# Ends of the two mixture-of-experts layers: a fifth gather buffer, an earlier first scaling, and a last expert tile handled in two column halves

## The reference, cut to what matters

```python
for l in range(DEPTH):                                  # DEPTH = 2
    ...                                                 # attention, residual
    hp = modulate(rms_norm(xp, norm_ffn[l]), sh_m_p, sc_m_p)
    hs = modulate(rms_norm(xs, norm_ffn[l]), sh_m_s, sc_m_s)
    xp = xp + gt_m_p[:, None, :] * hier_moe(hp, *moe_prm)
    xs = xs + gt_m_s[:, None, :] * hier_moe(hs, *moe_prm)
y_prompt = rms_norm(xp, final_norm)
y_sample = rms_norm(xs, final_norm)
```

```python
hid = silu(x @ w_gate[e]) * (x @ w_up[e])               # per expert, width 256
out = sum over the two chosen experts of e_w * (hid @ w_down[e])
```

## Time and profile before

| what | value |
|---|---|
| time, median of 3 executions | 1373.82 us (1367.92 to 1375.38) |
| profiled execution, own time | 1371.09 us |
| its span, first to last instruction | 1369.3 us |
| PE busy in the span | 1256.3 us (92%) |
| DVE, ACT, POOL busy | 583.9, 418.2, 55.8 us |
| mean granted TensorE clock | 0.967 |
| records | 16486 |

### The profile page before, as it was taken

The page is one execution under the profiler, slowest core; times in us unless marked ns, Lnnn a source line. Parts: engine busy times, 40 slices in busy tenths (PEclk is TensorE's granted clock), DMA queues, the critical chain, the costliest instruction groups (busy, mean ns, idle before and its releaser), DMA issues.

```text
span 1369.3 us, 16486 instructions
## 1 busy us (share of the span) xinstructions
PE 1256.3 (92%) x5449; PEld 660.8 (48%) x5449; DVE 583.9 (43%) x1334; ACT 418.2 (31%) x843; POOL 55.8 (4%) x64
## 2 busy tenths in 40 slices
PE   5899899999999999999939996999999999998884
PEld 2455566666664464444414443555444554443331
DVE  1322355444553664222236446677725642212215
ACT  2332344444451121111122336667621211111113
POOL 0102000000000120000020000000000100000002
PEclk9999999999999999999969997999999999999997
DMA  9969999422253067999970004000030469999945
GB/s 375 397 240 414 408 410 414 171 94 94 94 195 134 31 275 263 384 382 371 340 292 9 0 0 190 2 1 1 25 132 31 190 229 374 355 345 343 346 178 216
DMA packets 78545, 299.44 MB, mean 219 GB/s; under 512 B 11817, under 2 KB 29932, under 8 KB 62988
## 3 DMA queue, kind: packets, MB, share of 16 engines
q1 hardware_dynamic: 48096, 206.46, 41.1%
q0 software_dynamic: 16640, 64.56, 12.1%
q10 hardware_dynamic: 13740, 27.52, 5.5%
HBM read 223.79 MB, written 74.73 MB: 218 GB/s over the span
## 4 chain that ended last, share of the span: by engine, by line
PE 76%; SPq 8%; DMA 4%; issue 4%; DVE 4%; ACT 2%; ACTq 1%; DVEq 1%; POOL 1%; POOLq 0%
PE ps L1916 14%; PE ps L1588 10%; PE ps L1573 10%; PE ps L1528 8%; PE ps L1933 6%; PE ps L1806 6%; SPq L468 4%; PE ps L1769 4%; PE ps L1968 3%; PE ps L1621 3%; PE ps L1647 3%; PE ps L1871 2%; PE ps L1543 2%; DMA arena<-in_ada_w 2%; PE ps L1762 2%
## 5 line engine op out<-in xcount | busy, mean ns | idle before, releaser
L1916 PE MATMUL ps<-arena 128*128 128x512 f32 x560 | 246.2, 593 | 0.0
L1528 PE MATMUL ps<-const,arena 128*128 128x128 f32 (+2 forms) x1000 | 157.9, 286 | 58.3 <-DVE arena L1025 19.9
L1528 PEld LDWEIGHTS ps<-const,arena 128*128 128x128 f32 (+2 forms) x1000 | 118.4, 144 | 138.0 <-issue 34.8
L1077 DVE TENSOR_REDUCE hst<-ps 128x1 f32<-128x640 f32 (+1 forms) x160 | 114.7, 717 | 126.3 <-PE ps L1806 89.0
L1573 PE MATMUL ps<-arena 128*128 128x512 f32 (+2 forms) x400 | 156.3, 548 | 8.1 <-DVE arena L1036 4.8
L1916 PEld LDWEIGHTS ps<-arena 128*128 128x128 f32 x560 | 103.9, 190 | 117.2 <-issue 117.1
L690 ACT ACTIVATE arena<-ps 128x640 f32<-128x640 f32 (+1 forms) x160 | 98.9, 618 | 183.9 <-PE ps L1528 169.8
L1588 PE MATMUL ps<-arena 128*128 128x512 f32 x320 | 142.0, 597 | 1.4 <-issue 1.4
L1933 PE MATMUL ps<-arena 128*128 128x512 f32 x280 | 126.1, 593 | 2.2 <-ACT arena L789 2.2
L695 ACT ACTIVATE arena<-ps,hst 128x640 f32<-128x640 f32 (+1 forms) x160 | 112.6, 704 | 20.1 <-DVE hst L1077 19.9
L1573 PEld LDWEIGHTS ps<-arena 128*128 128x128 f32 x400 | 76.4, 195 | 81.6 <-issue 63.9
(11 more groups left out here) (201 smaller groups left out, 1102.0 us busy)
## 6 DMA issues: line engine op xcount, KB each, us to landing
arena<-in_ada_w SPq DMA_DIRECT2D x62, 768.0 KB, 11.4
slot_rows<-arena POOLq DMA_DIRECT2D x10, 4096.0 KB, 66.2
arena<-in_moe_w_down SPq DMA_DIRECT2D x35, 1024.0 KB, 17.8
arena<-in_moe_w_gate SPq DMA_DIRECT2D x31, 1024.0 KB, 9.2
arena<-in_moe_w_up SPq DMA_DIRECT2D x31, 1024.0 KB, 12.7
slot_rows<-arena ACTq DMA_DIRECT2D x35, 512.0 KB, 8.0
arena<-slot_rows SPq DMA_DIRECT2D x124, 128.0 KB, 11.4
arena<-in_moe_fed SPq DMA_DIRECT2D x8, 1024.0 KB, 9.5
```

The costliest lines, as they stand in the source:

```text
L1077: nc.vector.tensor_reduce(hst[:, b:b + 1], scores(s, step(s)[3]), AX.XY, ALU.max, negate=True)\
L1528: return nc.tensor.transpose(out, in_, ident[0:rows, 0:rows])
L1916: last = mm(split(bank(gu_bank(u)), 2), e_xsT[:, nth(u, D)][:, k * P:(k + 1) * P], w[:, k], start=k == 0, stop=k == KD - 1)
```

## The change

- `e_g` has five buffers. The fifth lies in the ring region that the down weights of slot 1 use; POOL no longer waits for `combined` ahead of tile 4's gathers.
- The first gather of tile 0 counts on a semaphore of its own, `gathered_first`. ACT's scale 0 waits for that one alone; DVE waits for the second gather ahead of combine 0. SP's wait at L552 is for the second gather of tile 0.
- The last expert tile of each layer is handled by `last_y_out`: PE signals `half_y` after the first column half of the last `down`; ACT copies and stores column half 0, then column half 1. `last_stored` is counted four times instead of three.
- At the start: PE's wait for the cleared banks goes (DVE's clearing stays), and the two weights' semaphores become one.

```diff
-    e_g = [ar(2 * D * b, 2 * D) for b in range(4)]
+    e_g = [ar(2 * D * b, 2 * D) for b in range(4)] + [ring(SLOT + HALF_SLOT, 2 * D)]
+    def gathered(t, c):
+
+        return S("gathered_first" if t == c == 0 else f"gathered{t}")
+
+    def gathers(l, t):
+        return (32 if t else 16) * (l + 1)
...
-        load(S("uk_landed"), w_uk, A["mla_w_uk"], 2)
-        load(S("uv_landed"), w_uv, A["mla_w_uv"], 2)
+        load(S("ukv_landed"), w_uk, A["mla_w_uk"], 2)
+        load(S("ukv_landed"), w_uv, A["mla_w_uv"], 2)
...
             if b == 1:
-                sp.wait_ge(S("gathered0"), 32)
+                sp.wait_ge(gathered(0, 1), gathers(0, 0))
...
-            pool.wait_ge(S("last_stored"), 16 * RING_N * (l + 1))
+            pool.wait_ge(S("last_stored"), 16 * (RING_N + 1) * (l + 1))
             for t in range(NTILE):
-                if t >= 4:
-
-                    pool.wait_ge(S("combined", l), t - 3)
                 for c in range(2):
                     pool.indirect_dma_start(
-                        e_g[t % 4][:, c * D:(c + 1) * D], None, slots,
+                        e_g[t][:, c * D:(c + 1) * D], None, slots,
                         bass.IndirectOffsetOnAxis(ap=slot_i[:, 2 * t + c:2 * t + c + 1], axis=0))\
-                        .then_inc(S(f"gathered{t % 4}"), 16)
+                        .then_inc(gathered(t, c), 16)
...
-            act.wait_ge(S(f"gathered{t % 4}"), 32 * (2 * l + t // 4 + 1 if t % 4 == 0 else l + 1))
-            a = e_g[t % 4][:, 0:D]
+            act.wait_ge(gathered(t, 0), gathers(l, t) if t else 16 * (l + 1))
+            a = e_g[t][:, 0:D]
...
+            def last_y_out(t, u, r):
+                row = act.value_load(first_row[0:1, ds(t, 1)], min_val=0, max_val=SPARE_ROW)
+                act.wait_ge(S(f"y_stored{u % RING_N}", l), r * 16 + 16)
+                y = e_y[:, nth(u, D)]
+                for n, done in enumerate((S("half_y"), S("y_done", l))):
+                    act.wait_ge(done, t + 1 if n else l + 1)
+                    act.activation(y[:, n * BANK:(n + 1) * BANK], bank(6 + n), ACT.Copy).then_inc(S("y_out", l), 1)
+                    act.wait_ge(S("y_out", l), t + 2 + n)
+                    act.dma_start(slots[ds(row, P), n * BANK:(n + 1) * BANK], y[:, n * BANK:(n + 1) * BANK]).then_inc(S("last_stored"), 16)
+
...
-                y_out(R * RING_N + k, k, R + k // RING_N, k >= SLOT_TILES - LOOPED - RING_N)
+                if k + 1 < SLOT_TILES - LOOPED:
+                    y_out(R * RING_N + k, k, R + k // RING_N, k >= SLOT_TILES - LOOPED - RING_N)
+                else:
+                    last_y_out(R * RING_N + k, k, R + k // RING_N)
...
-        nc.vector.memset(ps[:, 5 * BANK:8 * BANK], 0.0).then_inc(S("parts_cleared"), 1)
+        nc.vector.memset(ps[:, 5 * BANK:8 * BANK], 0.0)
...
             dve.wait_ge(S("scaled"), NTILE * l + t + 1)
-            a, b = e_g[t % 4][:, 0:D], e_g[t % 4][:, D:2 * D]
+            if t == 0:
+                dve.wait_ge(gathered(0, 1), gathers(l, 0))
+            a, b = e_g[t][:, 0:D], e_g[t][:, D:2 * D]
...
-        pe.wait_ge(S("parts_cleared"), 1)
...
-        pe.wait_ge(S("uk_landed"), 32)
-        pe.wait_ge(S("uv_landed"), 32)
+        pe.wait_ge(S("ukv_landed"), 64)
...
+                    if n == 0 and u == SLOT_TILES - 1:
+                        last.then_inc(S("half_y"), 1)
...
                 if t == LAT - 1:
-                    pe.wait_ge(S("last_stored"), 16 * RING_N * 2)
+                    pe.wait_ge(S("last_stored"), 16 * (RING_N + 1) * 2)
```

More of the change, by code:

```diff
@@ L1984, in last_sums @@
                 pe.wait_ge(S("gated"), t + 1)
-                part(t, e_g[t % 4][:, 0:D], False).then_inc(S("combined", 1), 1)
+                part(t, e_g[t][:, 0:D], False).then_inc(S("combined", 1), 1)
                 if t == 1:
```

## The result

| | before | changed kernel |
|---|---|---|
| median | 1373.14 us | 1357.21 us |
| lowest to highest of 9 executions | 1367.33 to 1375.38 us | 1346.46 to 1366.24 us |
| profiled execution, own time | 1371.09 us | 1348.28 us |
| its span | 1369.3 us | 1346.4 us |

The ratio is 0.9896, interval 0.9854 to 0.9937: 14.3 us faster where 7.5 us were forecast.

The account below looks back on a forecast made before the run. PE, busy 92% of the span, was taken as the bound except at the layer ends. Savings of 2.45 us in layer 0 and 5.08 us in layer 1 sum to 7.5 us, forecast 1365.5 us, range 1359 to 1372 us.

Parts of the forecast that it names:

- over most of the run only PE's work counts: Whole kernel: PE, busy 92% of the span, sets the time except at the two layer ends where it runs dry.
- The base: Time the gain is subtracted from: 1372.05 us, the average of three runs and the profiled one, giving 1364.5 us.
- s: Both layer ends: time by which splitting the last tile's copy and store advances the gathers, 1.24 us layer 1, 1.67 layer 0.
- The third rival: Last tile's two half stores stand behind each other; gain only 5.8 us, 1367.2 us; chance 0.12.
- Fifth buffer: End of layer 1: tile 4's gathers follow at once, removing a 2.53 us stall; worth nothing in layer 0.
- the fourth rival: End of layer 1: the added gather buffer gives nothing, gathers land late; gain 4.5 us, 1368.5 us; chance 0.12.
- Part 4 on the full clock: End of layer 1: PE's part for tile 4 takes 1.9 us instead of 3.68, gaining 1.3 us.
- The second rival: End of layer 1: PE runs part 4 at the lower clock again; gain 6.2 us, 1366.8 us; chance 0.16.
- Early scaling: Tile 0's first rows scaled on landing: 0.78 us in layer 0, nothing by itself in layer 1.
- Layer 0's 2.45 us: End of layer 0: 0.78 us from scaling plus 1.67 us from the half stores, counting in full before PE's next work.
- the fifth rival: Layer 1's attention: the shift puts PE at the lower clock in more stretches; slower, near 1374.5 us; chance 0.05.
- The start: Kernel start: dropping PE's wait for cleared banks and merging the weights' semaphores costs and gains nothing.

Follow-up runs that it names:

- light loads: Kernel before and changed kernel, a quarter of each down weight loaded from the fourth tile on: 1348.46 and 1342.48 us; first chip 1349.35 and 1342.29 us.
- the 19 matmuls: Unused matmuls added behind layer 0's last `down`: changed kernel 1342.44 us, again 1347.51 us; kernel before 1350.61 us; changed kernel with reduced weight loads 1341.26 us.

## Why the prediction was wrong

The measured median, 1357.21 us, lies under the range of 1359 to 1372 us. **The step that failed** is the first: "over most of the run only PE's work counts". It was read from PE's 92% of the whole span. In the second half of layer 1's tiles the loads set the pace, in the trace of before already: twelve of 17 transposes had DVE idle ahead of them until rows landed, and the timeline has such a tile, which I hadn't opened:

```profile
1308.34 2.02 DVE L1442 STREAM_TRANSPOSE arena<-arena 128x1024 f32<-128x1024 f32 x1 [9.31 <-DMA arena<-slot_rows]
...
1310.72 0.44 PE L1528 MATMUL ps<-const,arena 128*128 128x128 f32 x2 [1.85 <-DVE arena L1448]
```

From that followed the second fault, "which nothing but such stretches explains in the rows": I put the spread of three executions down to PE's clock and gave it 3 us at either side. Over 114 executions the kernel before ranged from 1345.56 to 1385.77 us (standard deviation 8.4). A median of nine can be off by several us, and the ratio of two with it. The base was off as well: I averaged four executions to 1372.05 us, and the mean of the 114 is 1368.5. The paired comparisons together, 61 executions of before (mean 1368.6) and 27 of the changed kernel (mean 1360.0), give 8.6 +/- 3.9 us. The forecast of 7.5 lies within; the 14 us of the first comparison don't need another cause than the loop's own spread, and its trace has most of its surplus there.

**Point by point.**
- *Halves.* s was 0.89 us in layer 1 and 1.82 in layer 0, forecast 1.24 and 1.67: 2.71 together instead of 2.91. The half store landed in 2.5 us and 2.0 us; I took 2.2. The issues of the changed kernel's line L807, in layer 1 and then in layer 0:

```profile
DMA to landing us min/median/max: 2.5/2.5/2.5
```

```profile
DMA to landing us min/median/max: 2.0/2.0/2.0
```

The rule of the Trainium skill, "DMA: Bandwidth & Descriptors", section on the anatomy of one DMA, gave 2.6 us by my estimate: near the one, 0.6 above the other. The page gives that rule for transfers that POOL issues; these are ACT's. The third rival, stores behind each other, didn't occur.
- *Fifth buffer.* The tenth gather landed 5.5 us after its issue (forecast 6.09), and root 1 wasn't held up; the fourth rival falls. DVE's waits in 1309 to 1346 us of the changed kernel (idle us in all, times, longest) have no stall left behind the first tiles:

```profile
DVE arena L1501 <- DMA arena<-slot_rows,slot_i: 15.6, 1, 15.6
DVE rstd L1035 <- ACT st L628: 1.3, 5, 0.3
DVE arena L1501 <- ACT arena L678: 1.0, 1, 1.0
```

- *Part 4 on the full clock.* Forecast 1.9 us behind a pause of 1.5; measured 1.98 behind 1.43. The second rival falls.
- *Early scaling.* Its 0.78 us in layer 0 held (0.71 alone). "In layer 1 this edit is worth nothing by itself" was wrong: I looked at combine 1, not at POOL, whose wait for the buffer hangs on tile 0. With the fifth buffer there it is right, so the sum of the whole was not hurt.
- *Layer 0's 2.45 us, "in full".* From the last `down` to the projection there were 24.57, 24.80 and 24.44 us in three traces of the kernel before and 22.50, 21.71, 21.81, 21.65 and 22.04 in five of the changed one: 2.7 us less in the mean. PE's low clock reached 3.2 to 3.6 us into the projection before and 2.8 to 6.0 us in the changed kernel, and at the first scores about 1 us seemed given back: the stretch up to there took 123.3 us in the mean of the same three and 124.3 in that of the five. But the next stretch, to the first gate-up of layer 1, took 273.6 us in the three and 270.6 in the five. From the first projection to that point the granted clock stood at 0.50 for 34.0 to 34.4 us before and for 29.9 to 34.9 us in the changed kernel. So the fifth rival, more time at the lower clock, didn't occur; in the mean there were 3 us less. From the last `down` of layer 0 to the first gate-up of layer 1 the mean fell from 421.4 to 416.8 us, 4.6 us where 2.45 were forecast: of these, 2.0 us came behind the pause, with the clock, and I had no term for them. The traces' sum is 4.6 + 4.4 = 9.0 us from three and five traces; the times with light loads say 7.1 +/- 1.7, those with full loads 8.6 +/- 3.9.
- *The start.* "Costs and gains nothing" isn't contradicted: up to layer 0's first gate-up 14 traces with the edits there took 511.3 us in the mean (506.0 to 514.7), six without them 512.5 (509.0 to 515.4).

## What to carry to other kernels

Before a 92% busy engine is called the bound, take the distance between iterations from the trace at the start and at the end of each loop, and compare the bytes of an iteration over that distance with the rate that the loop reaches: a loop with PE at full busy in one half can be bound by loads in the other. Where such a loop stands between two small edits and the clock on the wall, measure the edits with its loads lightened in both kernels; here that cut a range of 37 us to 8 and resolved 7 us. When a shift changes where PE's clock is low, add up both clock levels to a point far behind the shift: at the first scores it looked like a loss of 1 us, at the next gate-up it was a gain of 2. Edits that each remove the same stall don't add: leave one out of the whole as well as putting it in alone.

## What the runs showed of the hardware that was not expected

- With a DMA share of 1.03 to 1.04 throughout, the rate in the late stretch of the same loop was 330 to 371 GB/s in different executions. The slowest trace is that of the fifth buffer alone:

```profile
1240.00:1290.00 50.00, 38.66 (x95) 16.68 (x94) 10.98 (x12) 5.62 (x8) 0.00 (x0) 1.00 1.04 330
```

The share doesn't tell a fast loop from a slow one; the GB/s of this late stretch do (in 1160 to 1200 us they were 365 and 364 in the slower trace of before and the faster one of the changed kernel). The sign that comes first is the wait for a tile's rows: in the traces in which PE pauses in this loop it had grown to between 7.8 and 10.5 us by the first pause.
- 16.5 us of idle matmuls some 400 us ahead of the loop went with a loop of 198.87 us in every trace (three with full loads): DVE's waits for rows began at the eleventh or twelfth of the 17 transposes there, and at the fifth to seventh in the twelve full-load traces without them. The mechanism is open, and so is how often it holds.
- With a pause of 17 to 20 us ahead of them 12 transposes of layer 1 took 2.82 us in both kernels, at the lower clock, and 1.53 us behind the 19 matmuls, whose own time lay in PE's idle stretch. In two of the three traces with these matmuls and full loads the clock fell again 3.5 and 3.1 us ahead of the projection and rose 3.4 and 3.7 us into it, and the transposes took 2.24 and 2.09 us. The trace with light loads:

```profile
683.29 16.47 PE L1975 MATMUL ps<-const 128*128 128x512 f32 x38
...
701.63 1.53 PE L1549 MATMUL ps<-const,arena 128*128 128x128 f32 x12 [1.87 <-DVE arena L1044]
```
